# The last gate block of four feed-forward stages: computed in two halves, with a reordered subtraction

## What is computed

```python
def swiglu(x, w_gate, w_up, w_down):
    return (jax.nn.silu(x @ w_gate) * (x @ w_up)) @ w_down

x = layer_norm(ALPHA * x + FFN_RESIDUAL * swiglu(x, ffn1_w_gate[l], ffn1_w_up[l], ffn1_w_down[l]),
               ln1_g[l], ln1_b[l])
```

## Time and profile before

| | |
|---|---|
| median of 3 runs | 960.83 us (960.59 to 961.72) |
| the profiled execution, own time | 960.22 us |
| its span, first to last instruction | 958.2 us |
| PE busy (matmul) | 947.7 us, 99% |
| DVE busy | 854.6 us, 89% |
| ACT busy | 632.0 us, 66% |
| mean granted TensorE clock | 0.998 |

### The profile page before, as it was taken

One profiled execution on the slowest core, in us unless ns is written; L12 is line 12 of the kernel. 1 busy time (PEld: TensorE's weight loads), 2 busy tenths in 40 slices (PEclk: granted clock), 3 DMA queues, 4 the chain that ended last, 5 costly groups with the idle time before them and its releaser, 6 DMA issues.

```text
span 958.2 us, 15318 instructions
## 1 busy us (share of the span) xinstructions
PE 947.7 (99%) x5418; PEld 817.7 (85%) x5418; DVE 854.6 (89%) x1121; ACT 632.0 (66%) x771; POOL 21.5 (2%) x53
## 2 busy tenths in 40 slices
PE   9999999999999999999999999999999999999996
PEld 9978888888788988888998888898887889888885
DVE  6999998966899999998999999988578989999986
ACT  6666665568884667675566767655678755767653
POOL 0000000001100000000000000000010000000000
PEclk9999999999999999999999999999999999999999
DMA  8576644572344655555636575554633445645554
GB/s 318 209 264 235 246 175 178 218 263 89 132 152 156 220 204 213 183 212 195 220 132 215 182 302 180 219 167 185 220 136 122 166 161 211 224 177 220 175 186 155
DMA packets 34653, 187.28 MB, mean 195 GB/s; under 512 B 3888, under 2 KB 3888, under 8 KB 19504
## 3 DMA queue, kind: packets, MB, share of 16 engines
q1 hardware_dynamic: 33120, 177.22, 51.4%
q0 software_dynamic: 1488, 9.45, 2.7%
HBM read 185.61 MB, written 1.05 MB: 195 GB/s over the span
## 4 chain that ended last, share of the span: by engine, by line
PE 93%; DVE 6%; issue 1%; ACT 0%; DVEq 0%; POOL 0%; POOLq 0%
PE bank L1594 68%; PE bank L1450 8%; PE bank L1452 8%; PE bank L1451 8%; PE bank L1513 1%; DVE xn L1000 1%; PE bank L1825 1%; DVE xn L1019 1%; DVE w_lo L947 1%; DVE w_lo L966 0%; DVE w_lo L904 0%; DVE qT L1034 0%; DVE stick_t L926 0%; DVE h_lo L1140 0%; DVE w_lo L954 0%
## 5 line engine op out<-in xcount | busy, mean ns | idle before, releaser
L1594 PE MATMUL bank<-xT,w_hi 128*128 128x512 f32 (+1 forms) x1248 | 397.2, 387 | 0.0
L1594 PEld LDWEIGHTS bank<-xT,w_lo 128*128 128x128 f32 x1200 | 223.2, 188 | 49.6
L1594 PE MATMUL bank<-xT,w_lo 128*128 128x256 f32 x1200 | 234.6, 278 | 0.0
L505 ACT ACTIVATE w_hi<-raw 128x2048 fp32r<-128x2048 f32 x116 | 221.7, 1911 | 1.6 <-DMA raw<-stream 1.6
L1594 PEld LDWEIGHTS bank<-xT,w_hi 128*128 128x128 f32 x1248 | 198.0, 189 | 6.0 <-issue 0.8
L904 DVE TENSOR_TENSOR w_lo<-raw,w_hi 128x2048 fp32r<-128x2048 f32 x54 | 123.5, 2287 | 10.1 <-ACT w_hi L505 9.9
L646 ACT ACTIVATE ez<-bank 128x512 f32<-128x512 f32 x64 | 38.4, 600 | 103.3 <-PE bank L1594 103.3
L1594 PE MATMUL bank<-w_hi,h_hi 128*128 128x512 f32 x252 | 98.5, 391 | 1.4 <-DVE h_lo L1140 1.4
L1594 PE MATMUL bank<-w_lo,h_hi 128*128 128x512 f32 x252 | 98.6, 391 | 0.0
L1594 PE MATMUL bank<-w_hi,h_lo 128*128 128x512 f32 x252 | 98.4, 391 | 0.0
L1450 PE MATMUL bank<-xT,w_hi 128*128 128x256 f32 x304 | 86.2, 284 | 0.0
(11 more groups left out here) (188 smaller groups left out, 1572.7 us busy)
## 6 DMA issues: line engine op xcount, KB each, us to landing
raw<-stream SPq DMA_DIRECT2D x110, 1024.0 KB, 4.8
raw<-stream SPq DMA_DIRECT2D x110, 512.0 KB, 4.5
lnp<-ln_gb POOLq DMA_DIRECT2D x6, 1024.0 KB, 5.3
band<-rel_band POOLq DMA_DIRECT2D x2, 1024.0 KB, 9.7
xn<-x POOLq DMA_DIRECT2D x1, 1024.0 KB, 6.9
out<-xn SPq DMA_DIRECT2D x4, 256.0 KB, 2.0
qT<-first SPq DMA_DIRECT2D x2, 384.0 KB, 4.0
kT<-first SPq DMA_DIRECT2D x2, 384.0 KB, 5.4
```

What stands on the lines that cost most here:

```text
L505: nc.scalar.activation(w_hi[:, at(slot if into is None else into)], raw[:, slot, :], ACT.Copy).then_inc(hi_ready, 1)
L1594: return nc.tensor.matmul(o, w, x, start=start, stop=stop, skip_group_check=True)
```

## The change

The last gate unit is computed by `gate_half` in two halves, with `rest` between them, in place of `columns` after `rest`. ACT copies each half out of the bank, DVE gets a `gate_sum`, and ACT's silu reads the sum instead of the bank. DVE's subtraction for unit 30 moves ahead of `gather` part 2. The index function for the gate semaphores counts one more step for each FFN.

```diff
         def wide_gate(l, f, j):
-            return (2 * l + f) * (SF - 2) + (j - 2)
+            return (2 * l + f) * (SF - 1) + (j - 2)
...
                 step(SF - 1, more=False)
                 split_hi(l, base + 3 * SF + 3, 0, first[0] + 1 + SF)
+                copy_gate(SF, 0)
 
                 act.wait_ge(unit_used, used(l, base + 3 * SF + 1))
                 act.wait_ge(hf_done, it(l, f, SF) + 1)
                 nc.scalar.activation(h_hi[:, 0:4, :].rearrange("p (c b) t -> p c b t", c=2), h_pair,
                                      ACT.Copy).then_inc(hhi_done, 1)
                 split_hi(l, base + 3 * SF + 4, 1, first[1] + 1 + SF)
-                silu(FP - 1, 3 * SF + 2)
+                copy_gate(SF, 1)
                 split_hi(l, base + 3 * SF + 5, 2, first[2] + 1 + SF)
+                silu_sums(SF)
...
                 up_sum(SF, 1)
+                split_lo(l, base + 3 * SF + 3, 0)
                 gather(l, f, 2)
-                split_lo(l, base + 3 * SF + 3, 0)
 
                 dve.wait_ge(hhi_done, it(l, f, SF) + 1)
...
                 gather(l, f, 3)
+                gate_sum(SF)
                 split_lo(l, base + 3 * SF + 4, 1)
                 split_lo(l, base + 3 * SF + 5, 2)
...
                 step_with_gate(SF - 1, stop=True)
+                gate_half(SF, 0)
                 rest(stop=True)
-
-                gate(SF)
+                gate_half(SF, 1)
                 pe.wait_ge(m_read, (2 * l + f) * 8 + 2)
                 columns(l, base + 3 * SF + 3, 0, M[1])
```

## The result

The changed kernel's median is 964.38 us (964.03 to 965.59, 7 runs), that of the kernel before, run beside it, 961.71 us (959.91 to 962.52, 7 runs). The ratio of the runs is 1.0038, 95% interval 1.0028 to 1.0048: slower by 3.7 us (2.7 to 4.6). The forecast was 2.3 us slower. The sign and the main mechanism were right, the size wasn't. The median of 964.38 still lies just inside the range of 961.4 to 964.6, but that range was counted from 960.83, and beside it the kernel before took 961.71: 1.0038 times 961.71 is 965.4, above the range. The profiled execution took 964.03 us with a span of 962.3, 4.1 more than before.

The account below looks back on a forecast made before the run. PE was taken to bound the kernel, with hl_lo from DVE just in time. 3 x (0.74 + 0.1) - 0.19 = +2.3 us, so a median of 960.83 + 2.3 = 963.1 us; range 961.4 to 964.6.

Parts of the forecast that it names:

- PE's own work: Gate in two halves: 5.56 us in place of 5.75, a gain of 0.19 us in each FFN, 0.77 in four.
- The cover of ACT's copy by `rest`: Between the gate halves: `rest` runs until 165.74, the copy until 165.4, a margin of 0.3 us, so no cost.
- DVE's queue: End of FFNs one to three: DVE delivers hl_lo 0.74 us later, and PE waits about 0.97 us.
- The first term of the sum: 3 x 0.74 - 0.19: hl_lo late by 0.74 us in three FFNs, less the gain kept in the last.
- (a): Rival: hl_lo's delay is partly taken up, 0.45 to 0.6 us in three FFNs; +1.2 to +1.6 us; chance 0.21.
- (b): Rival: hl_lo isn't what PE waits for, only PE's shorter gate counts; -0.77 us, 960.1; chance 0.11.
- (d): Rival: matmuls cost only their columns, so 16 fewer gain nothing; +2.5 us, 963.3; chance 0.54 together with the forecast.
- the load behind unit 31: End of FFNs one to three: later load issue stalls PE at the layer norm; 0.1 us each, bounds 0 to 0.4.
- rival (c): Load lands late in three FFNs, norm waits the full 0.4 us; +3.2, up to +3.9 us; 964.4; chance 0.12.
- own sign of being wrong: Prediction is wrong if the turn of x (line 1513) waits more than 0.4 us; one of three such signs.
- Rival (e): The wait lowers PE's clock from 2.4 to 1.2 GHz; up to 7.7 us three times, 984 at most; chance 0.02.

## Why the prediction was right and wrong

**Right.** PE's own work: 5.56 us for two halves, -0.20 in the last FFN where -0.19 stood. The cover of ACT's copy by `rest`: the copy runs from 164.58 to 165.18, the second half starts at 165.52. DVE's queue: idle 0.72 ahead of unit 30 (0.7 predicted), the idle 0.61 ahead of unit 32 gone, hl_lo at 177.02, and since this trace is 0.22 ahead, at 177.24 by the old clock, which is the predicted figure. PE's wait is 0.96 on three occasions (0.97 predicted), 0.73 net (0.74), the weight load's waits are 3.7 us (3.7). (The working once says that a result can be read 0.17 us behind PE; its rows and its sums have 0.20, and the copy's start at 164.58 is 0.20 behind PE's 164.38. And PE has a second long wait, 1.3 us for GpSimd, ahead of its first matmul; nothing hangs on it.) The first term of the sum, 3 x 0.74 - 0.19 = 2.0, holds to some hundredths. Rivals (a) and (b) fall with it; (d) falls as the last FFN did keep its 0.2.

**Wrong: the term "the load behind unit 31".** It was taken at 0.1 for each of three FFNs, with an upper bound of 0.4. The table gives 1.72, 1.24 and 0.83 less 0.73: 0.99, 0.51 and 0.10, together 1.6 where 0.3 stood and 1.2 was the most. With 1.6 in place of 0.3 the sum gives +3.6. So the true case lies beyond rival (c), which had the right mechanism, at a chance of 0.12. The prediction's own sign of being wrong, more than 0.4 us at the turn of x, appeared in FFN one with 0.9. The step had three faults.

First, the choice inside the bounds. I let the load take less "since it no longer follows close on the load of slot 0". The share of the DMA engines in 40 slices of 160 to 180 us, before, then after:

```profile
DMA  7998500000000044669994092499893899996898
```
```profile
DMA  9999000000000599799820000076599989999898
```

After, the engines are empty for 1.7 us ahead of the load's issue at 172.19; before, they are busy right up to it at 170.90, and then empty for half a microsecond. The load took 5.86 and not less; in four traces of the two kernels it took 5.5 to 5.9 in FFN one, 4.9 to 5.0 in FFN two and 4.7 to 4.8 in FFN three. The emptiness bought nothing there. With other orders of DVE's work the load of FFN one took 4.8 to 5.0 (issued at 170.5 to 171.4, or at 174.0 to 175.9) and once 7.0 (171.55).

What sets the long loads apart is in the traces. The program's own instructions are loaded too, by a queue of their own (q8, `instruction`), some 29 packets of 16 KB in each execution, each of which took 0.9 to 2.0 us. The DMA queues in the first 2 us behind the issue of this load (packets, MB, share of the 16 engines), in the changed kernel from 172.2 and with the sum behind unit 31 from 171.4:

```profile
q1 hardware_dynamic: 16, 0.13, 31.6%
q8 instruction: 1, 0.02, 5.1%
```
```profile
q1 hardware_dynamic: 20, 0.16, 41.8%
```

In the four traces of the two kernels and with the moved subtraction alone such a packet starts 0.5 to 1.0 us behind the issue, and the load took 5.5 to 7.0 us. In the other eight traces it starts 4.2 to 4.5 us behind the issue, or ahead of it, and the load took 4.8 to 5.0. Over all 1 MB loads that SP issues behind the first 30 us, in all 13 traces, the median is 5.9 us for the 100 with such a packet within 2 us, and 4.8 for the other 1291. So where this traffic falls goes with the load's time, and empty engines ahead of it didn't help; no run moves the packet alone, so that it is the cause isn't shown.

Second, the bound. It used one trace's 5.51 us as the most that the load can take. At 5.86 everything behind it is 0.35 later. That, and 0.09 from DVE's half of x to PE's matmul (185.51 + 0.71 = 186.22 against 186.31), which I had counted into the margin, turn 0.4 into 0.85; the measured wait in FFN one is 0.9.

Third, FFN one stood for two and three. For hl_lo it does; for the load not. In FFN two ACT was idle 0.61 ahead of line 525, the first turn of x lost 0.06, and 0.45 went later, in the products of the norm's rows; in FFN three 0.35 and nearly nothing. That the load and not some other stall is the cause is shown by the rows above (the norm behind line 968, that behind line 525, that behind the load) and by the sum behind unit 31: with the load issued 0.8 earlier, and landing 1.8 earlier in FFN one, 1.3 of those 1.6 us are gone from the ends of its trace, and the times have +1.7.

**Not foreseen: the clock.** Rival (e) didn't occur in the changed kernel: through waits of 0.96 the granted clock stayed at 2.4 GHz. It occurred in two experiments, behind waits of 2.2 and 3.3 us. The Trainium skill (TensorE: Matmul & The Clock Gate, The HAM clock gate) has the rate depend on how busy PE has been; the runs here agree with that, and since the same wait of 2.2 us had no fall in FFN one, the wait's length alone doesn't decide.

**Left open.** How much the stalls at block 2 add. PE's waits there in FFNs three and four are 0 and 0.4 us in the two traces of the kernel before, 0.5 and 0.6 in those of the changed one, 0.7 without the moved subtraction, 0.8 with it alone and 1.3 to 2.0 in the five kernels without GpSimd that make unit 31 ahead of `gate_sum`; that is one trace each, and in FFN three only kernels with the new gate show one. The load behind the stall in FFN four, issued 4.4 us ahead of PE's first product with `h_hi`, took 4.9 us in the three traces with the old gate and the old order, 5.9 with the moved subtraction alone, and 6.3 to 7.8 in all nine with the new gate; in those nine, and in no other, instruction packets start 1.4 to 2.8 us behind its issue. So the new gate very likely brings this stall, by where the instruction packets now fall; for FFN three the packets don't sort the traces as cleanly. The ends alone give 3.1 to 3.6 and the ratio 3.7 with an interval of 2.7 to 4.6, so the times don't need these stalls, and don't exclude them.

## What to carry to other kernels

When an engine's queue gets later, follow every semaphore that it raises, also the one that frees a buffer: here the late release of a slot cost nearly as much as the late operand. Price such a load with the spread of its time over several executions and each place for itself, since a margin of 0.3 us against a load that varied by 0.4 between two traces of one kernel is no margin. Look also at what else is loaded behind its issue. And a gain of 0.19 us on the bounding engine isn't one if it puts 0.6 us of work into the queue of an engine that has no gap there.

## What the runs showed of the hardware

- A 1 MB load at the same place of the program took 4.8 to 7.0 us (end of FFN one), and one of FFN four's first 4.9 to 7.8, in programs that differ in one gate's form, in the order of a few DVE instructions or in what GpSimd adds. The long ones go with a 16 KB packet of instructions that starts within some 3 us of the issue (FFN one: 5 traces with it 5.5 to 7.0, 8 without 4.8 to 5.0).
- GpSimd's additions cost DVE 1.1 us for each of three instructions beside them in one kernel (0.69, 2.29 and 1.22 us alone, 1.79, 3.38 and 2.31 beside them), 0.7 and 1.1 for two in the other (3.00 and 2.31), and GpSimd itself took 3.05 us for scaling 128x1024 in one kernel and 4.65 in the other.
- TensorE's granted clock fell to 1.2 GHz for about eight matmuls behind a wait of 2.2 us, in two of three places, and behind one of 3.3 us, again in two of three, and not behind waits of 1.8 us in six places of two kernels.
